# A block-wise convolution moved from VectorE into GpSimd's stream

## The reference

```python
def centred_depthwise_conv(u, w, b):
    s = u.shape[1]
    up = jnp.pad(u, ((0, 0), (CONV_LEFT, CONV_WIDTH - 1 - CONV_LEFT), (0, 0)))
    y = b
    for tap in range(CONV_WIDTH):
        y = y + up[:, tap:tap + s] * w[tap]
    return y

def rg_lru(u, w_r, b_r, w_i, b_i, lam, reverse):
    ub = u.reshape(bsz, s, LRU_BLOCKS, LRU_BLOCK_DIM)
    gate_r = jax.nn.sigmoid(jnp.einsum('bsni,nij->bsnj', ub, w_r).reshape(bsz, s, LRU_WIDTH) + b_r)
    gate_i = jax.nn.sigmoid(jnp.einsum('bsni,nij->bsnj', ub, w_i).reshape(bsz, s, LRU_WIDTH) + b_i)
    log_a = -LRU_C * gate_r.astype(jnp.float32) * jax.nn.softplus(-lam.astype(jnp.float32))
    a = jnp.exp(log_a)
    b = jnp.sqrt(-jnp.expm1(2.0 * log_a)) * (gate_i * u).astype(jnp.float32)
    _, h = lax.associative_scan(_linear_combine, (a, b), axis=1, reverse=reverse)
    return h
```

## Time and profile before

| | us |
|---|---|
| median of 3 runs | 3008.37 (3005.05 to 3008.74) |
| the profiled execution | 3007.21 |
| its span from first to last instruction | 3005.4 |
| PE busy in the span | 2962.6 (99%) |
| DVE busy | 1837.5 (61%) |
| ACT busy | 1521.0 (51%) |
| POOL busy | 507.6 (17%) |

### The profile page before, as it was taken

One profiled execution on the slowest core, in us unless ns is written; L12 is line 12 of the kernel. 1 busy time (PEld: TensorE's weight loads), 2 busy tenths in 40 slices (PEclk: granted clock), 3 DMA queues, 4 the chain that ended last, 5 costly groups with the idle time before them and its releaser, 6 DMA issues.

```text
span 3005.4 us, 37026 instructions
## 1 busy us (share of the span) xinstructions
PE 2962.6 (99%) x13268; PEld 2442.0 (81%) x13268; DVE 1837.5 (61%) x2461; ACT 1521.0 (51%) x2028; POOL 507.6 (17%) x1001
## 2 busy tenths in 40 slices
PE   8999999999999999999999999999999999999998
PEld 6888888888888778778888888888888887787887
DVE  6536655555465776876545555555556668786555
ACT  6535444444344566755434344445445547785433
POOL 0003302112033310013203021122321244010210
PEclk9999999999999999999999999999999999999999
DMA  7546666666667655556666666667776666666774
GB/s 259 169 153 210 211 198 191 211 194 211 195 209 225 207 172 164 158 169 211 203 199 205 198 207 197 200 199 229 232 212 187 189 203 195 193 207 203 243 253 155
DMA packets 330364, 603.21 MB, mean 201 GB/s; under 512 B 33376, under 2 KB 58336, under 8 KB 329440
## 3 DMA queue, kind: packets, MB, share of 16 engines
q1 hardware_dynamic: 293392, 541.13, 57.8%
q0 software_dynamic: 36240, 59.05, 6.1%
q10 hardware_dynamic: 576, 0.94, 0.1%
HBM read 561.15 MB, written 10.49 MB: 190 GB/s over the span
## 4 chain that ended last, share of the span: by engine, by line
PE 87%; DVE 6%; ACT 5%; issue 2%; DMA 1%; ACTq 0%; DVEq 0%
PE acc L1874 27%; PE acc L1876 27%; PE acc L1875 27%; ACT whi L972 2%; DVE wlo L1298 1%; DVE wlo L1303 1%; PE sd L1936 1%; PE sd L1956 1%; ACT prob L1209 1%; PE tp L1892 1%; PE tp L2037 1%; ACT qk L1217 0%; PE sd L1942 0%; PE tp L2027 0%; DMA raw<-in_w_mem_kv 0%
## 5 line engine op out<-in xcount | busy, mean ns | idle before, releaser
L1874 PE MATMUL acc<-whi,set_hi 128*128 128x512 f32 x4080 | 1610.3, 395 | 18.1 <-DVE wlo L1303 12.4
L1876 PE MATMUL acc<-whi,set_lo 128*128 128x512 f32 x4080 | 1591.0, 390 | 0.0
L1875 PE MATMUL acc<-wlo,set_hi 128*128 128x512 f32 x4080 | 1590.3, 390 | 0.0
L1303 DVE TENSOR_TENSOR wlo<-raw,whi 128x1024 fp32r<-128x1024 f32 x944 | 1135.6, 1221 | 704.3 <-ACT whi L972 702.4
L972 ACT ACTIVATE whi<-raw 128x1024 fp32r<-128x1024 f32 x944 | 980.5, 1058 | 871.5 <-PE acc L1876 700.1
L1874 PEld LDWEIGHTS acc<-whi,set_hi 128*128 128x128 f32 x4080 | 767.1, 188 | 192.4 <-DVE wlo L1303 19.5
L1876 PEld LDWEIGHTS acc<-whi,set_lo 128*128 128x128 f32 x4080 | 766.7, 188 | 161.6
L1875 PEld LDWEIGHTS acc<-wlo,set_hi 128*128 128x128 f32 x4080 | 767.1, 188 | 157.1 <-issue 1.9
L939 POOL DMA_DIRECT2D u<-u x704 | 344.1, 497 | 1564.8 <-DVE u L1426 1374.6
L1298 DVE SCALAR_TENSOR_TENSOR wlo<-raw,par,whi 128x512 fp32r<-128x512 f32 x160 | 111.6, 747 | 47.1 <-ACT whi L975 46.3
L975 ACT ACTIVATE whi<-raw,par 128x512 fp32r<-128x512 f32 x160 | 104.3, 715 | 22.7 <-PE acc L1876 11.1
(11 more groups left out here) (250 smaller groups left out, 1321.0 us busy)
## 6 DMA issues: line engine op xcount, KB each, us to landing
raw<-in_w_ff SPq DMA_DIRECT2D x512, 512.0 KB, 4.5
raw<-in_w_in SPq DMA_DIRECT2D x248, 512.0 KB, 4.4
raw<-in_w_out SPq DMA_DIRECT2D x96, 512.0 KB, 4.2
u<-u POOLq DMA_DIRECT2D x704, 32.0 KB, 4.3
raw<-in_w_mem_kv SPq DMA_DIRECT2D x32, 512.0 KB, 4.7
raw<-in_w_proj_a SPq DMA_DIRECT2D x32, 512.0 KB, 4.2
raw<-in_w_proj_b SPq DMA_DIRECT2D x32, 512.0 KB, 6.1
raw<-in_w_kv SPq DMA_DIRECT2D x48, 256.0 KB, 3.4
```

What stands on the lines that cost most here:

```text
L1303: V.tensor_tensor(wlo[:, c], raw[:, c], whi[:, c].bitcast(f32), ALU.subtract).then_inc(w_lo, 1)
L1874: T.matmul(o, h[:, tok], whi[:, c], start=first, stop=False)
L1875: T.matmul(o, h[:, tok], wlo[:, c], start=False, stop=False)
L1876: ins = T.matmul(o, l[:, tok], whi[:, c], start=False, stop=last)
```

## The change

The convolution of each block leaves DVE's stream (four instructions on 128x256 for a block: one `tensor_scalar`, three `scalar_tensor_tensor`) and stands in POOL's stream at p-3. POOL makes the three later taps as a product into a small buffer `tap` and an addition, so there are seven instructions a block, each behind the one before by a semaphore (`conv_step`), save the second, which reads nothing of the first. `conv(n)` on POOL waits for `lru_ok` of block n-2, since that block read the same half of `xhs`. `lru_square` on DVE gains a wait on `conv_ok`.

```diff
-        sc.at("dve", p - 1, "conv", n)
+        sc.at("pool", p - 3, "conv", n)
...
+        tap = kv[:, LB * UTW + 8 * P + 2 * TOK:LB * UTW + 8 * P + 3 * TOK]
...
+            def conv(n):
+
+                pool.wait_ge(sm["tail_hi"], sc.info["ut"] + n // 4 + 1)
+                pool.wait_ge(sm["tail_lo"], sc.info["ut"] + n // 4 + 1)
+                pool.wait_ge(sm["ut_pad"], 1)
+                pool.wait_ge(sm["att_lo"], NJOB)
+                if n:
+                    pool.wait_ge(sm["conv_ok"], n)
+                if n >= 2:
+                    pool.wait_ge(sm["gates_pe"], n - 1)
+                    pool.wait_ge(sm["lru_ok"], n - 1)
+                xh = xhs[:, TOK * (n % 2):TOK * (n % 2 + 1)]
+                base = UTW * n
+                pc = PCOL["convw"] + 4 * n
+                nc.gpsimd.tensor_scalar(xh, ut[:, base:base + TOK], par[:, pc:pc + 1],
+                                        par[:, PCOL["convb"] + n:PCOL["convb"] + n + 1], ALU.mult,
+                                        ALU.add).then_inc(sm["conv_step"], 1)
+                steps = 0
+                for k in range(1, 4):
+                    nc.gpsimd.tensor_scalar(tap, ut[:, base + k:base + k + TOK], par[:, pc + k:pc + k + 1], None,
+                                            ALU.mult).then_inc(sm["conv_step"], 1)
+                    steps += 2
+                    pool.wait_ge(sm["conv_step"], 6 * n + steps)
+                    nc.gpsimd.tensor_tensor(xh, xh, tap, ALU.add)\
+                        .then_inc(sm["conv_step" if k < 3 else "conv_ok"], 1)
+                    if k < 3:
+                        pool.wait_ge(sm["conv_step"], 6 * n + steps + 1)
...
-            def conv(n):
...
-                link(V.tensor_scalar(xh, ut[:, base:base + TOK], par[:, pc:pc + 1],
-                                     par[:, PCOL["convb"] + n:PCOL["convb"] + n + 1], ALU.mult, ALU.add))
-                for k in range(1, 4):
-                    ins = V.scalar_tensor_tensor(out=xh, in0=ut[:, base + k:base + k + TOK],
-                                                 scalar=par[:, pc + k:pc + k + 1], in1=xh,
-                                                 op0=ALU.mult, op1=ALU.add)
...
             def lru_square(n):
...
+                dve.wait_ge(sm["conv_ok"], n + 1)
```

More of the change, by code:

```diff
@@ L648, in build @@
                  "pool_mix", "pool_mid", "pool_mm", "pool_hi", "pool_lo",
-                 "conv_ok", "gates_pe", "gates_ok", "lru_sq", "lru_root", "lru_ok",
+                 "conv_step", "conv_ok", "gates_pe", "gates_ok", "lru_sq", "lru_root", "lru_ok",
                  "lru_hi", "lru_lo", "lruc_ok", "lexp_ok",
@@ L941, in _ @@
             steps = dict(shuffle=shuffle, pool_w=pool_w, mem_again=mem_again, x_spill=x_spill, gate_store=gate_store,
-                         gate_load=gate_load, merge_store=merge_store, merge_load=merge_load, lru_w=lru_w,
+                         gate_load=gate_load, merge_store=merge_store, merge_load=merge_load, lru_w=lru_w, conv=conv,
                          x_back=x_back)
@@ L1650, in lru_const @@
                 V.memset(pad[:, :, UTW - 1:UTW], 0.0).then_inc(sm["ut_pad"], 1)
-            def conv(n):
[L1653 to L1661, removed]
-                link(V.tensor_scalar(xh, ut[:, base:base + TOK], par[:, pc:pc + 1],
-                                     par[:, PCOL["convb"] + n:PCOL["convb"] + n + 1], ALU.mult, ALU.add))
-                for k in range(1, 4):
-                    ins = V.scalar_tensor_tensor(out=xh, in0=ut[:, base + k:base + k + TOK],
-                                                 scalar=par[:, pc + k:pc + k + 1], in1=xh,
-                                                 op0=ALU.mult, op1=ALU.add)
-                    if k < 3:
-                        link(ins)
-                ins.then_inc(sm["conv_ok"], 1)
             def lru_square(n):
@@ L1776, in _ @@
                          dif_smx=dif_smx, dif_prob=dif_prob,
-                         pool_lo=pool_lo, lru_const=lru_const, conv=conv,
+                         pool_lo=pool_lo, lru_const=lru_const,
                          lru_square=lru_square, lru=lru, lru_lo=lru_lo,
```

## The result

| | before | after |
|---|---|---|
| median of 7 runs, us | 3006.66 (3005.05 to 3008.74) | 3016.38 (3015.84 to 3017.92) |
| ratio | | 1.0032, interval 1.0022 to 1.0043 |
| the profiled execution, us | 3007.21 | 3017.35 |
| its span, us | 3005.4 | 3015.5 |

What follows compares the result with a forecast made beforehand. The circle of ACT and DVE was taken to cause PE's gaps in the recurrence, PE being busy nearly throughout. Terms: 3007.2 - 1.8 + 0 + 3.5 = 3008.9, plus 1.2 to the median, 3010.1 us; range 3004 to 3020.

Steps and rivals of the forecast that it cites:

- full exclusion: DVE stands while a POOL instruction runs; for the convolutions of n = 1, 2 and 4 this would cost 13.8 us.
- The circle of ACT and DVE: Recurrence, 2500 to 2742: ACT and DVE wait for each other, leaving PE 9.9 us of waits on `wlo`.
- Term 1: At n = 2, taking the convolution off DVE lets `wlo` start sooner: -1.8 us; the other 15 convolutions are hidden.
- The price on POOL: Seven POOL instructions a convolution at 0.66 us each: 4.6 us, bounds 3.0 to 8.6.
- room of an ordinary block: Time for POOL's convolution before it runs beside DVE's next `wlo` and squares: 5.6 us in one block, 4.4 in another.
- rival 1: Engines exclude each other and POOL is slow, from about 0.7 us an instruction; 3025 us at 0.8; chance 0.21.
- within 6 us: Sign that the forecast is right: POOL's seven instructions of a convolution take no more than 6 us.
- Term 3: POOL's arithmetic slows DVE at n = 1, 2 and 4: +3.5 us, a quarter of full exclusion.
- Term 2: PE's gates: POOL's convolution is in time, short stalls replace later gaps; 0, bounds 0 to +3 us.
- rival 2: PE waits at the gates for the convolution or a slow ISA start; 3020 us for a 20 us start; chance 0.07.
- Rival 3: The convolution is on the circle after all; up to 9.9 us of PE's waits go, 2998.5 us; chance 0.05.

Runs made afterwards that it cites:

- e3_no_conv: Kernel before with the convolution left out on both DVE and POOL, PE's gates not waiting for it: 3004.34 us, ratio 0.9994.
- e7_scan_early: Kernel before with DVE's scans at p+6 for p+7, ahead of one `wlo`, convolution still on DVE: 2994.78 us, ratio 0.9962.
- e1_early: Changed kernel with POOL's convolution two slabs sooner (p-5 for p-3), ahead of the shuffles of n = 1 and n = 4: 3012.98 us, ratio 1.0020.
- the shadow: Kernel before, DVE's convolution kept, plus a copy of POOL's seven instructions whose result nobody waits for: 3017.07 us, ratio 1.0036.
- The memsets: Kernel before, DVE's convolution kept, plus 14 POOL fills of `tap` a block that read nothing and nobody waits for: 3007.30 us, ratio 1.0003.
- short products: Changed kernel with products written as product plus 0.0: 3008.42 us at p-3; 3006.66 us with the convolution at p-5.

## Why the prediction was right or wrong

As a change, the forecast was 3010.1 - 3008.4 = +1.7 us; measured are +9.7. Its base, the median of three runs, was itself 1.7 us above the median of seven (3006.66). The range holds the time, but in part by luck: its upper end was three convolutions at full exclusion, and nearly half of the loss came from blocks that were said to lose nothing.

**What bounds the kernel: right.** The circle of ACT and DVE sets the pace from 2500 to 2742. e3_no_conv (DVE's hidden work away: 2.0 us) and e7_scan_early (the scans one `wlo` sooner: 12.1 us) are its two proofs.

**Term 1, -1.8 us: right.** 2.0 us by the medians, 1.7 in the table, at the one block named; the other 15 convolutions were hidden as argued. That step was read from the idle time ahead of `wlo`, and it holds. By the times alone the 2.0 us are not clear of noise.

**The price on POOL, 4.6 us: wrong, and the step on which the rest turned.** Alone, the first instruction takes 0.55, a product 0.92 and an addition 0.74 us. Seven of them with their semaphores are 0.55 + 3 x 1.84 = 6.1 us, 0.87 each. The room of an ordinary block had been counted as 4.4 to 5.6 us and the threshold as about 0.7 us an instruction, so the case of rival 1 was met. The nearest row I leaned to was POOL's time to issue a transfer, which has nothing to do with arithmetic; the bounds themselves (0.43 to 1.23 us) had the threshold inside them, and that should have weighed more than the value between. With the meetings a convolution takes 7.8 to 11.6 us, 9.1 on the mean, and "within 6 us" failed in every block. The Trainium skill's figure (GPSIMD Engine Reference, Performance versus the Vector engine), from which 0.56 us was worked out, is too low for the addition here, 0.73 to 0.74; the measurement decides.

**Term 3, +3.5 us: the mechanism right, the size wrong.** From e3_no_conv to e1_early, where the place in the queue costs least, the contact costs 2.0 + 6.7 = 8.7 us; the shadow alone, which also meets DVE's own convolution, gives 10.8. A quarter of full exclusion was argued from shuffles that ran at one length beside two loads of DVE. The memsets show what was wrong with that row: POOL can work beside DVE's `wlo` and squares without touching them as long as it doesn't read, so a row of transfers could not stand for arithmetic that reads. And the ordinary blocks were said to lose nothing, by a room for 4.6 us; they hold some 4.7 us of the loss in the table, by the squares at 1219 ns (median). The sentence of the Trainium skill (SBUF — State Buffer, Who interferes with whom) that two such instructions block each other whole is what the runs agree with: 1.35 and 2.15 us for 0.55 and 0.92, 1.23 for 0.685. With it term 3 gave 3020; measured were 3016. The prediction looked at two inputs alone; the runs show the same for DVE instructions with one, 1.22 us for 0.69 in `stage_a` at 2499.63 of the kernel after.

**Term 2, 0 with bounds to +3: wrong in size, at its upper bound.** The rule behind it, that such a stall only takes the place of later gaps, failed. The waits were 2.78 and 2.75 us, because the convolution of n = 1 took 11.6 us (2488.71 to 2500.30) and that of n = 4 9.1 (2543.14 to 2552.24), where 4.6 had been put in. The first went on into ACT (2.6 us at L1238, then 3.2 at `whi`), so into the circle. Moving the convolution ahead of the shuffles gives 3.0 us back; with short products hardly anything is left to give (1.2, within noise). Its base, that ACT does not wait for PE, was a statement on the kernel before.

**Rivals.** Rival 1 is what happened, with 0.4 to 0.6 us a block where it had 0.8, and from the threshold that it named. Of rival 2 the waits at the gates came, at n = 1 and n = 4, but not the dear start: the instruction of the kind ISA takes 42 ns and the first convolution starts 0.13 us behind the shuffle (2466.81 and 2466.68). Rival 3 fell with e3_no_conv.

The sum with the measured terms: 3006.7 - 2.0 + 8.7 + 3.0 = 3016.4. The terms are differences of medians in a chain that ends at after, so the sum must close; what it shows is the shares. What stays open: how much of the 8.7 falls to the three exposed convolutions and how much to the ordinary ones is known from the table alone (e1_early: 0.9 and 4.7 us of growth up to and behind n = 4, on top of the 1.7 that its start should have gained), and no run had POOL's work in ordinary blocks only.

## What to carry to other kernels

Ask of work to be moved whether it is on the chain that waits at all: here 29 of its 31 us lay beside idle time of DVE, so there was next to nothing to gain, and the same reading of the waits showed the place on the circle where another order paid 12 us. An instruction of GpSimd that reads is not free beside VectorE: add to its own length that of the VectorE instructions it will stand behind, and compare the sum with the time until the next VectorE instruction that somebody waits for: here every block that went past it paid 0.4 to 0.7 us. Where a price is unknown and such a threshold lies between its bounds, forecast the two sides of the threshold and not a value in the middle.

## What had not been expected of the hardware

- A product of 128x256 on GpSimd with one operation takes 0.92 us, and with two (times, plus 0.0) 0.48; the addition of two tiles 0.74. The profile's spans on GpSimd are rough, but the kernel's time moved with them. The cause of the first is not known; it was worth 6 to 8 us here.
- GpSimd's 14 writes of a tile without reading it left VectorE's instructions with two inputs alone (5.28 us beside `wlo` of 1.22 us), but not its copy with one (0.63 us for 0.42 at 2501.77). The copy at 2557.31 is as long, and there GpSimd was issuing transfers (2556.27 to 2558.24).
- Behind the stall of 2.78 us PE's granted clock fell: the stretch 2500 to 2505 has 0.66 of full speed (clock is the third number from the end), which is the mean of some time at 1.2 and some at 2.4 GHz, and the next one has 1.00 again.

```profile
2500.00:2505.00 5.00, 4.65 (x14) 3.79 (x15) 4.96 (x8) 2.32 (x6) 4.87 (x6) 0.66 0.65 173
2505.00:2510.00 5.00, 5.00 (x24) 4.09 (x23) 2.64 (x3) 3.25 (x6) 4.64 (x6) 1.00 0.24 91
```

PE's busy time is 3.4 us longer than before because of such stretches. In this part of the kernel they partly stand in for gaps that PE would have had. One place shows it: the kernel before has a gap of 1.79 us at 2609.57 and a granted clock of 0.50 (1.2 GHz) from 2610 to 2612; e3_no_conv has a gap of 1.80 at the same step (2606.32), a clock of 1.00 from 2600 to 2628, and a gap of 1.22 at 2623.22 that the kernel before has not. That such stretches cost nothing in the kernel after is argued and not shown.
